# Attention, output projection and routing woven into the expert loop

## The reference

```
h  = modulate(rmsnorm(x))
x += gate1 * W_out [ mLSTM heads || windowed attention heads with sinks ]     # "mixer"
h2 = modulate(rmsnorm(x))
q  = h2 @ w_q                       # 8 heads x 256
scores of 128 + 128 keys per head -> top 16 of each -> top 16 of the 256 sums -> expert ids, softmax gates
x += gate2 * sum over 8 heads, 16 experts of  gate * gelu(h2 . u[id]) * v[id]
```

## Time and profile before

| | |
|---|---|
| median of 3 runs | 4431.73 us (the lowest 4428.21) |
| profiled execution, its own time | 4423.65 us |
| its span, first to last instruction | 4421.8 us |
| work before the first gather | 1386 us |
| expert loop | the 3035 us after it |
| read and written in DRAM | 1348 MB |

### The profile page before, as it was taken

How to read it: one execution, slowest core, us unless ns; L and a number is a source line. 1 busy time by engine, 2 the same in 40 slices (tenths; PEclk the granted TensorE clock), 3 DMA queues, 4 the chain that set the end, 5 groups by cost and what they waited for, 6 DMA issues and landing times.

```text
span 4421.8 us, 41953 instructions
## 1 busy us (share of the span) xinstructions
PE 2957.5 (67%) x11157; PEld 1284.8 (29%) x11157; DVE 2402.1 (54%) x5728; ACT 826.1 (19%) x2523; POOL 1578.3 (36%) x1434
## 2 busy tenths in 40 slices
PE   8899778888863656656656655755755755755555
PEld 1444366555542212212312311311311411411111
DVE  1232354333316774674674684684684684685554
ACT  1111123323311111111111111111111111111111
POOL 0000011101102454454454454454554454455453
PEclk9899887777677878877877877877978977967777
DMA  9101133111134999999999999999999999999998
GB/s 368 56 34 41 59 101 114 39 43 47 38 130 189 418 415 390 420 409 389 420 404 391 420 408 391 420 404 391 416 408 402 409 395 408 409 404 406 403 420 368
DMA packets 220971, 1348.41 MB, mean 305 GB/s; under 512 B 23370, under 2 KB 34250, under 8 KB 71370
## 3 DMA queue, kind: packets, MB, share of 16 engines
q0 software_dynamic: 165888, 1208.03, 67.1%
q1 hardware_dynamic: 47212, 113.48, 7.4%
q10 hardware_dynamic: 7776, 25.96, 1.5%
HBM read 1316.04 MB, written 31.33 MB: 305 GB/s over the span
## 4 chain that ended last, share of the span: by engine, by line
DMA 37%; PE 12%; issue 10%; DVE 7%; POOL 3%; ACT 1%; POOLq 0%; SPq 0%; DVEq 0%; ACTq 0%
DMA pe_ring<-arg_uv,pe_fetch_idx 34%; PE pe_acc L1357 10%; POOL pe_ring L1311 3%; DMA pe_h<-h_scratch 2%; DVE pe_ring L1550 2%; PE pe_qP L1335 2%; ACT pe_diag L1423 1%; DVE pe_w L1555 1%; DMA pe_w_q<-arg_w_q 0%; DVE pe_rest L1514 0%; DVE pe_pos L1480 0%; DVE pe_ab L1517 0%; DVE pe_scores L1492 0%; DVE pe_rest L1511 0%; ACT pe_gelu L1418 0%
## 5 line engine op out<-in xcount | busy, mean ns | idle before, releaser
L1357 PE MATMUL pe_acc<-pe_ring,pe_diag 128*64 128x512 f32 x4608 | 1527.5, 799 | 1220.6 <-ACT pe_diag L1423 1220.6
L1311 POOL DMA_INDIRECT pe_ring<-arg_uv,pe_fetch_idx x1152 | 1391.4, 1208 | 1554.8 <-PE pe_acc L1357 1304.7
L1550 DVE CUSTOM_DVE_ANT_0 pe_ring<-pe_ring,pe_h 128x1024 f32<-128x1024 f32 x1152 | 1405.6, 1225 | 850.0 <-DMA pe_ring<-arg_uv,pe_fetch_idx 777.2
L1357 PEld LDWEIGHTS pe_acc<-pe_ring,pe_diag 128*64 128x64 f32 x4608 | 344.8, 167 | 2294.4 <-ACT pe_diag L1423 1809.4
L1418 ACT ACTIVATE pe_gelu<-pe_dot 128x2 f32<-128x2 f32 x576 | 117.1, 203 | 1876.9 <-DVE pe_dot L1550 1876.8
L1423 ACT ACTIVATE pe_diag<-pe_pick,pe_w 128x64 f32<-128x64 f32 x1152 | 337.9, 340 | 606.0 <-DVE pe_w L1555 606.0
L351 PE MATMUL in_z<-w_in,in_hT 128*128 128x512 f32 (+1 forms) x864 | 356.8, 576 | 22.3 <-ACT in_hT L381 22.3
L1335 PE MATMUL pe_qP<-pe_h2T,pe_w_q 128*128 128x128 f32 x2304 | 298.5, 285 | 29.3 <-DMA pe_w_q<-arg_w_q 29.3
L1335 PEld LDWEIGHTS pe_qP<-pe_h2T,pe_w_q 128*128 128x128 f32 x2304 | 273.8, 196 | 139.4 <-issue 139.4
L351 PEld LDWEIGHTS in_z<-w_in,in_hT 128*128 128x128 f32 x864 | 168.3, 196 | 205.7 <-issue 198.0
L1555 DVE TENSOR_TENSOR pe_w<-pe_gelu,gates 128x2 f32<-128x2 f32 x576 | 92.1, 160 | 189.0 <-ACT pe_gelu L1418 117.9
(11 more groups left out here) (256 smaller groups left out, 2418.4 us busy)
## 6 DMA issues: line engine op xcount, KB each, us to landing
ada_w<-arg_w_ada SPq DMA_DIRECT2D x12, 2048.0 KB, 10.3
pe_ring<-arg_uv,pe_fetch_idx POOLq DMA_INDIRECT x1152, 11.6
w_in<-arg_w_in SPq DMA_DIRECT2D x8, 1416.0 KB, 21.0
ml_qkT<-qkT_scratch SPq DMA_DIRECT2D x18, 512.0 KB, 3.5
pe_h<-h_scratch SPq DMA_DIRECT2D x36, 256.0 KB, 12.7
pe_w_q<-arg_w_q SPq DMA_DIRECT2D x8, 1024.0 KB, 12.9
ada_x<-arg_x ACTq DMA_DIRECT2D x9, 512.0 KB, 6.4
in_xn<-arg_x SPq DMA_DIRECT2D x9, 512.0 KB, 3.8
```

The costliest lines, as they stand in the source:

```text
L1311: pool.indirect_dma_start(out=ring[j][:], out_offset=None, in_=io.uv, in_offset=bass.IndirectOffsetOnAxis(ap=idg[half][:, j:j + 1], axis=0 ...
L1357: mm = pe.matmul(acc[b][cg * TOKS:(cg + 1) * TOKS, :], diag[:, j, :], ring[j][:, D + b * 512:D + (b + 1) * 512], start=False, stop=False)
L1550: dve.tensor_tensor_reduce(out=ring[j][:, 0:D], in0=ring[j][:, 0:D], in1=h2[i % NC][:], scale=1.0, scalar=0.0, op0=ALU.mult, op1=ALU.add, ...
```

## The change

`attend` and `peer` become one block, `mix_and_experts`. Every engine's work is written as three generators: `mixer(t)`, cut in 19 steps, `route(t)`, in up to 44 steps, and `pair(t, r)`. One function, `drive`, orders them alike on every engine: mixer 0 alone; then routing of tile 0 with one step of mixer 1 or 2 behind each of its first 38 steps; then the expert tiles, where behind each pair comes a step of the next tile's routing and, if `due` says so, one step of a mixer. `due` holds for three pairs in four of expert tiles 0 and 1 (48 steps each) and for every pair of tile 2, in which the last 18 of the 114 steps run. Everything is unrolled; `mlstm` is too.

The mixer steps, as PE and DVE have them (number 0 to 18): 0 scores of heads 0 and 1; then for each pair of heads, steps 1-2, 3-4, 5-6 and 7-8, first turn both and multiply the first by the values, then multiply the second and score the next two heads (none in step 8), while DVE masks and takes the maximum of the next two heads in steps 2, 4 and 6; 9 the attention's mix on DVE; 10 turning the mix; 11 to 14 four matmuls each of the output projection, with DVE's residual in 12 and 14; 15 and 16 the norm; 17 and 18 the two turns to h2T and h2.

Further edits: for tiles 0 to 3 `w_q` is not resident but streamed, a 512 KB column chunk of 512-byte runs per query into two buffers, and it is loaded whole in tile 2 behind the last mixer. The gate values are multiplied into the selection matrices ahead, for 8 slots at once on DVE, so that ACT's scale by GELU is the only step between dots and PE. Scores and turned probabilities share PSUM banks. The mLSTM outputs, the o gate and the gate rows go through DRAM. Keys are stored once, not twice; `mh_g` is folded into `w_out` on DVE before the block starts. The zero matmuls around a tile are gone. SP's `route(t+1)`, which loads the next h2T, comes behind `begin(t)`.

```diff
-def attend(nc, g, io):
...
-def peer(nc, g, io):
...
+def mix_and_experts(nc, g, io):
...
+    SUBS = 19
+    STEPS = 44
+    WQ = 2
+    STREAMED = 4
+    def due(t, r):
+        return (t < 2 and r % 4 != 3) or t == 2
+    def drive(begin, pair, end, mixer, route):
+        subs = chain.from_iterable(mixer(t) for t in range(TILES))
+        for _ in range(SUBS):
+            next(subs)
+        steps = route(0)
+        for k in range(STEPS):
+            next(steps, None)
+            if k < 2 * SUBS:
+                next(subs)
+        for _ in steps:
+            pass
+        for t in range(TILES):
+            begin(t)
+            steps = route(t + 1) if t + 1 < TILES else iter(())
+            for r in range(PAIRS):
+                pair(t, r)
+                next(steps, None)
+                if due(t, r):
+                    next(subs, None)
+            for _ in steps:
+                pass
+            end(t)
...
+            @block.sync
+                def chunk(m):
+                    if m < NSIDE * STREAMED:
+                        if m >= WQ:
+                            sp.wait_ge(s_qd, m - WQ + 1)
+                        i = m % NSIDE
+                        src = io.w_q[:, i * P:(i + 1) * P].rearrange("(k p) n -> p k n", p=P)
+                        sp.dma_start(wq[m % WQ][:], src).then_inc(s_wq[m % WQ], 16)
+                def route(t):
+                    if t:
+                        sp.wait_ge(s_qd, t * NSIDE)
+                    sp.wait_ge(s_hTo, t * 16 + 16)
+                    sp.dma_start(hq2T[:].rearrange("p k n -> p (k n)"), g.h2T_dram[t]).then_inc(s_hT, 16)
+                    for k in range(NSIDE):
+                        chunk(t * NSIDE + k + WQ)
+                        yield
...
+                def begin(t):
...
+                    if t:
+                        sp.wait_ge(s_out, t)
+                        sp.dma_start(io.y[t - 1], xo[:]).then_inc(s_st, 16)
...
+                        sp.wait_ge(s_st, t * 16)
+                    sp.wait_ge(s_x1o, t * 16 + 16)
+                    sp.dma_start(xo[:], g.x1_dram[t]).then_inc(s_xi, 16)
...
+            @block.gpsimd
+                def pair(t, r):
+                    n = t * PAIRS + r
+                    if n >= DEPTH:
+                        pool.wait_ge(s_acc, n - DEPTH + 1)
...
+            @block.tensor
+                def mixer(t):
...
+                    score(0)
+                    score(1)
+                    yield
+                    for i in range(4):
+                        turn(2 * i)
+                        turn(2 * i + 1)
+                        values(2 * i)
+                        yield
+                        values(2 * i + 1)
+                        if i < 3:
+                            score(2 * i + 2)
+                            score(2 * i + 3)
+                        yield
...
+                    for half in range(2):
+                        for k in range(KD):
+                            mm = pe.matmul(ST[half][:], mixT[:, k, :], w_out[:, k, half * 512:(half + 1) * 512],
+                                           start=(k == 0), stop=(k == KD - 1))
+                            if k == 3:
+                                yield
+                        mm.then_inc(s_wo_mm, 1)
+                        yield
...
+                def pair(t, r):
+                    pe.wait_ge(s_diag, t * PAIRS + r + 1)
...
+                    mm.then_inc(s_acc, 1)
...
+            @block.scalar
+                def mixer(t):
...
+                    for i in range(4):
+                        for h in (2 * i, 2 * i + 1):
+                            act.wait_ge(s_nm, t * AH + (h + 1))
+                            act.activation(s[h % 2][:], s[h % 2][:], ACT.Exp, bias=nmx[:, h:h + 1],
+                                           accum_out=rs[:, h:h + 1]).then_inc(s_p, 1)
...
+                        for h in (2 * i, 2 * i + 1):
+                            act.wait_ge(s_pTp, t * AH + (h + 1))
...
+                            act.activation(pT[h % 2][:], ST[h % 2][:], ACT.Copy).then_inc(s_pT, 1)
...
+                            yield
...
+                def pair(t, r):
...
+                    act.wait_ge(s_dot, (n + 1) * NC)
+                    act.activation(gelu[:, sl], dot[:, sl], ACT.Gelu_apprx_tanh).then_inc(s_gelu, 1)
+                    act.wait_ge(s_fill, n * NC // FILL + 1)
+                    act.wait_ge(s_gelu, n + 1)
+                    for i in range(sl.start, sl.stop):
+                        last = act.activation(wsel[:, i, :], wsel[:, i, :], ACT.Copy, scale=gelu[:, i:i + 1])
+                    last.then_inc(s_diag, 1)
...
+            @block.vector
+                def mixer(t):
...
+                    def scored(h):
+                        dve.wait_ge(s_sc, t * AH + (h + 1))
...
+                    scored(0)
+                    scored(1)
+                    yield
+                    for i in range(4):
...
+                        yield
+                        if i < 3:
+                            scored(2 * i + 2)
+                            scored(2 * i + 3)
+                        if i == 1:
+                            ca.link(dve.reciprocal(sg[:], sg[:]))
...
+                        yield
...
+                def pair(t, r):
...
+                    if (r * NC) % FILL == 0:
...
+                        dve.tensor_tensor(wsel[:, lo:lo + FILL, :], pick[:].unsqueeze(1).to_broadcast([P, FILL, TOKS]),
+                                          gates[t % 2][:, r * NC:r * NC + FILL].unsqueeze(2).to_broadcast([P, FILL, TOKS]),
+                                          ALU.mult).then_inc(s_fill, 1)
...
```

More of the change, by code:

```diff
@@ L1 @@
 from contextlib import ExitStack
-from itertools import chain, repeat
+from itertools import chain
 import numpy as np
@@ L585, in _ @@
                 sp.dma_start(io.new_kv, g.new_kv[:]).then_inc(s_out, 16)
-                with sp.Fori(1, TILES) as t:
+                for t in range(1, TILES):
                     load(t)
@@ L651, in _ @@
                 step(0, True)
-                with pool.Fori(1, TILES) as t:
+                for t in range(1, TILES):
                     step(t)
@@ L714, in _ @@
                 step(0, c_new, True)
-                with pe.Fori(1, TILES) as t:
+                for t in range(1, TILES):
                     step(t, c_run)
@@ new lines, in pair, with end @@
+                def pair(t, r):
+                    pass
+                def end(t):
+                    if t == TILES - 1:
+                        sp.wait_ge(s_out, TILES)
+                        sp.dma_start(io.y[t], xo[:]).then_inc(s_st, 16)
+                        sp.wait_ge(s_st, TILES * 16)
+                for cg in range(AKV):
+                    half = slice(cg * ADH, (cg + 1) * ADH)
+                    sp.dma_start(ckT[half, :], io.cache_kT[half, cg, :]).then_inc(s_small, 16)
@@ L1091, in _, with end @@
+                def end(t):
+                    pass
+                drive(begin, pair, end, mixer, route)
             @block.vector
             def _(dve):
-                def front(t, work):
-                    first = isinstance(t, int) and t == 0
-                    c = Count(dve, s_front, FRONT, t)
-                    dve.wait_ge(s_hs, t + 1)
-                    c.link(dve.tensor_reduce(hr[:], hq[:].rearrange("p (h n) -> p h n", h=MH), AX.X, ALU.add))
-                    dve.tensor_scalar(hr[:], hr[:], 1.0 / P, EPS, ALU.mult, ALU.add).then_inc(s_hm, 1)
-                    dve.wait_ge(s_q, t * 32 + 32)
-                    for h in range(AH):
+                ca = Count(dve, s_att)
@@ L1585, in _ @@
-                tile(0, 0)
-                with dve.Fori(1, TILES - 1) as t:
-                    tile(t, 1)
-                tile(TILES - 1, 1, more=False)
+                dve.wait_ge(s_const, 2)
+                dve.wait_ge(s_wo, 16 * KD)
+                dve.wait_ge(s_small, 96)
+                for k in range(KD // 2):
+                    last = dve.tensor_scalar(w_out[:, k, :], w_out[:, k, :], mhg[:, k:k + 1], None, ALU.mult)
+                last.then_inc(s_wom, 1)
+                drive(begin, pair, end, mixer, route)
```

1012 lines of the change are left out of this document (455 added, 557 removed).

## The result

The changed kernel takes 4463.8 us (median of five runs, 4457.2 to 4468.2) against 4431.7 for the kernel before: a ratio of 1.0073, with a 95% interval of 1.0057 to 1.0089. It is 32 us slower, where I had forecast 90. In the profiled executions the spans are 4465.9 and 4421.8 us, a difference of 44.

What follows compares the result with a forecast made beforehand. The expert loop was taken as DMA-bound, with 1386 us ahead of it in which no gather runs. Terms -373 + 415 + 20 + 25 + 3 = +90 gave 4522 us as median, range 4250 to 4690.

Steps and rivals of the forecast that it cites:

- the chain of waits: Tiles 0 to 2: DVE waits for PE's pair in nine of 19 mixer steps; one mixer takes 159 us, not 95.
- the +3 for the gates: Gates, h and o going through DRAM, with their DMA issues: +3 us (-5 to +15).
- The lost gate product on DVE and the zero matmuls lie beside DMA in tiles 3 to 8: 0: Tiles 3 to 8: removing this work gains 0 us, and these tiles stay at 337 us.
- The h2T load: Between tiles, seven times: h2T's load behind y's store makes PE's first query late, +25 us (0 to 40).
- The weave: Tiles 0 to 2: mixer steps between pairs cost +163, +157 and +95 us, together +415.
- The streamed chunks: The three streamed copies of w_q pass while DMA has room: 0 us (to 60).
- w_q loaded whole: Tile 2: w_q's 8 MB pass at DMA-bound time, 410 GB/s, +20 us (0 to 25).
- Saved in front: From attend's first load to the first gather: 292 us instead of 665, so 373 us saved.
- Rival (a): Tiles 0 to 2: the weave is hidden, 4117 us, or 4320 if half hidden; chance 0.2.
- Rival (b): Woven tiles: PE works at full clock, weave costs about 310, total 4390 us; chance 0.15 for 4343 to 4440.
- Rival (c): Streamed w_q chunks of short runs land after 20 us or more and become the bound: 4760 us; chance 0.15.
- Rival (d): Mixers: a table switch costs twice 1.28 us where ACT is busy, +54, 4576 us; chance 0.05.

Runs made afterwards that it cites:

- e9: Changed kernel with SP's load of the next h2T moved ahead of the h2 loads and y's store: 4431.5 us, ratio 1.0003.
- e6: Changed kernel loading only an eighth of each streamed w_q chunk from the second copy on: 4411.4 us, ratio 0.9966.
- e5: Changed kernel with all mixers ahead of the expert loop and only an eighth of each w_q chunk loaded from the second copy on: 4501.8 us, ratio 1.0170.
- e10: Changed kernel with exponentials and roots in the mixers of tiles 3 to 8 replaced by linear functions, so ACT keeps its GELU table: 4443.7 us, ratio 1.0033.
- e2: Changed kernel with DVE's mixer steps one position behind PE's in the expert loop: 4279.3 us, ratio 0.9658.
- e3: Changed kernel with a mixer step only every third pair, in all tiles, and w_q streamed for seven tiles: 4624.6 us, ratio 1.0429.
- e11: Changed kernel with a mixer step every third pair, w_q streamed for seven tiles, an eighth of each chunk from the second copy on: 4328.9 us, ratio 0.9761.
- e1: Changed kernel with all nine mixers ahead of the first gather and w_q still streamed in full chunks: 4652.6 us, ratio 1.0499.

## Why the prediction was wrong

The direction and the chain of waits held, the size didn't: +90 forecast, +44 in the profiled executions, +32 by the medians (the profiled execution lies 8 us under the median before and 4 over it after). By the table of stretches 27 of the missing 46 us lie in tiles 3 to 8 and 19 in tiles 0 to 2; the 3 us missed in front and the +3 for the gates cancel.

- **"The lost gate product on DVE and the zero matmuls lie beside DMA in tiles 3 to 8: 0".** This step failed, and it makes the larger part of what is missing. Tiles 3 to 8 with the end take 2030.7 us before, 2028.8 after and 2006.8 in e9. So the removed work was worth 24 us, and the late h2T load 22; in the changed kernel they cancel. I argued from a DMA share of 1.00 that nothing off DMA could matter. The gate product is the largest known piece, 1.8 of 4.3 us a tile, and the three removed pieces together are 2.1; half of the gain has no cause yet. That a shorter way from dots to a free buffer is what pays is argued, not shown.
- **The h2T load, +25.** This term was about right: e9 gives 31, of which 22 in tiles 3 to 7.
- **The weave, +415.** Measured +416, but this is luck: two errors nearly cancel in it, and it also holds the whole `w_q` of the next item. The mixers alone are worth 346 (e6 against e5), so I had over-sized the chain by 69; 36 of these are table loads (54 charged, 18 measured in e10). The streamed chunks, which I took at 0 (to 60), make up 58 (the changed kernel against e6); taking them at nothing failed too. The mechanism is shown by e2: one position of distance between DVE and PE, 184 us.
- **w_q loaded whole, +20.** This term held, at some 14; that tile 2 takes 94 us more and not 115 is mainly the chain. SP issues the load behind the last mixer step, where the tile is DMA-bound again:

```profile
2202.39 4.16 SPq L1072 DMA_DIRECT2D rt_w_q<-arg_w_q  x8
```

Pairs 18 to 31 take 84 us there and 70 in tile 3, by the two windows

```profile
2194.00:2278.00 84.00, 40.19 (x118) 10.02 (x120) 57.26 (x163) 11.54 (x44) 28.96 (x26) 0.70 0.99 404
2544.00:2614.00 70.00, 39.92 (x122) 9.69 (x120) 57.15 (x162) 11.54 (x43) 30.90 (x28) 0.78 1.01 421
```

Pairs 0 to 17, with the 18 mixer steps, take 173 us against 90, so the chain costs 83 in this tile, not 95.

- **Saved in front, -373.** Measured -370. Two errors cancel in it: the blocks ahead end 26 us later (the new block's first load at 746.8 instead of 720.6; I had given their edits nothing), and the block needs 269 us to the first gather, not 292. By the first instructions on each block's tiles `project_in` starts 6 us later and takes 13 more, and `mlstm` takes 7 more; what slows them wasn't tried. Two sums of this term are loose, too: the parts named for its 24 us add to 21, and those of a pair of heads to 10.4, not 9.7.
- **Rival (a)** fell: e3 and e11 show that even one step in three positions is not hidden. **Rival (b)** fell by the clock. **Rival (c)** had the mechanism: in e1 a chunk lands after 16.6 us (for "20 or more"), in tiles 0 and 1 of the changed kernel after 10.3. The chain covers two thirds of its cost: 164 us alone, 58 in the changed kernel. **Rival (d)** is out; table loads cost less than I charged, not double.

## What to carry to other kernels

When a second stream of work is woven into an in-order loop, let each consumer run one position behind its producer: the sums of busy time say whether it fits, the distance between the engines' steps says whether it is hidden, and here that one shift turned 0.7% slower into 3.4% faster. Bytes at DMA's rate priced a load in long runs fairly (the whole `w_q`: priced at 20 us, worth 14) and one in short runs at a third of its cost (the chunks: 51 us by their bytes, worth 164 with nothing to cover them), so a stream of short runs is priced by its landing and by who waits for it. A wait priced in one kernel may be missing from a difference because something else was taken away. Before calling a stall hidden by a buffer ring, estimate the ring's spare time by running it one shorter, and look where in the tile the stall falls.
